# Rotary embedding of the first block's attention: the exchange of halves by a permutation product, or by transfers within SBUF

## The reference, cut to what matters

```python
def apply_rotary(t, cos, sin):
    c = cos[:, :, None, None, :]
    sn = sin[:, :, None, None, :]
    tf = t.astype(jnp.float32)
    t1, t2 = jnp.split(tf, 2, axis=-1)
    return jnp.concatenate([t1 * c - t2 * sn, t2 * c + t1 * sn], axis=-1).astype(t.dtype)

def diff_attention(q, k, v, lam):
    ...
        scores = jnp.einsum('bqhcd,bkhcd->bhcqk', q[:, q_lo:q_hi], k[:, :q_hi],
                            preferred_element_type=jnp.float32) * scale
        ...
        probs = jax.nn.softmax(jnp.where(causal, scores, -jnp.inf), axis=-1)
        weights = probs[:, :, 0] - lam * probs[:, :, 1]
        outs.append(jnp.einsum('bhqk,bkhe->bqhe', weights.astype(v.dtype), v[:, :q_hi]))
```

## Time and profile before

| | |
|---|---|
| median of three executions | 3582.28 us |
| span of the profiled execution | 3593.5 us (the page gives no time around the span) |
| PE busy | 3218.1 us, 90% |
| DVE busy | 1427.9 us, 40% |
| ACT busy | 1130.1 us, 31% |
| attention of the first block | about 30 to 300 us of the span |
| 134 to 212 us, three heads | PE 26.00 of 26.00 us in each, at granted clock 1.00 |

### The profile page before, as it was taken

How to read it: one execution, slowest core, us unless ns; L and a number is a source line. 1 busy time by engine, 2 the same in 40 slices (tenths; PEclk the granted TensorE clock), 3 DMA queues, 4 the chain that set the end, 5 groups by cost and what they waited for, 6 DMA issues and landing times. The chain is left out here.

```text
span 3593.5 us, 42107 instructions
## 1 busy us (share of the span) xinstructions
PE 3218.1 (90%) x16329; PEld 2285.4 (64%) x16329; DVE 1427.9 (40%) x2352; ACT 1130.1 (31%) x1954; POOL 282.2 (8%) x280
## 2 busy tenths in 40 slices
PE   7999999999597877887885989899999998979999
PEld 5777888878333333333334857778887856868887
DVE  6772567743420000000003665443323557353332
ACT  4673676742100000000003243232223334232222
POOL 0000332200000000000000001300000000400000
PEclk9999999999799999999997997999999997989999
DMA  5222222222999999999996200033323300023332
GB/s 119 60 66 77 71 71 71 71 74 97 366 425 428 427 428 427 427 428 427 428 424 181 65 12 4 15 98 94 98 96 92 92 12 4 1 88 94 99 96 93
DMA packets 356679, 606.19 MB, mean 169 GB/s; under 512 B 72416, under 2 KB 306688, under 8 KB 331776
## 3 DMA queue, kind: packets, MB, share of 16 engines
q1 hardware_dynamic: 346544, 592.69, 44.8%
q0 software_dynamic: 9216, 8.42, 0.7%
q10 hardware_dynamic: 720, 2.36, 0.2%
HBM read 605.49 MB, written 23.07 MB: 175 GB/s over the span
## 5 line engine op out<-in xcount | busy, mean ns | idle before, releaser
L1839 PE MATMUL ex_up<-ex_W,ex_XT 128*64 128x512 f32 x1024 | 259.6, 665 | 80.9 <-DMA ex_W<-in_w_expert_up_dram 80.9
L237 ACT ACTIVATE f_hi<-f_raw 128x1024 fp32r<-128x1024 f32 x148 | 157.0, 1061 | 539.9 <-PE ff_bk L297 539.6
L1839 PE MATMUL ex_gp<-ex_W,ex_XT 128*64 128x512 f32 x1024 | 236.7, 616 | 52.1 <-DMA ex_W<-in_w_expert_gate_dram 50.6
L295 PE MATMUL ff_bk<-h_b_hi,f_hi 128*128 128x512 f32 x704 | 276.6, 393 | 2.8 <-DVE h_b_lo L3768 2.8
L296 PE MATMUL ff_bk<-h_b_lo,f_hi 128*128 128x512 f32 x704 | 276.2, 392 | 0.0
L297 PE MATMUL ff_bk<-h_b_hi,f_lo 128*128 128x512 f32 x704 | 275.9, 392 | 0.0
L246 DVE TENSOR_TENSOR f_lo<-f_raw,f_hi 128x1024 fp32r<-128x1024 f32 x148 | 180.8, 1223 | 231.6 <-ACT f_hi L237 231.6
L1868 PE MATMUL ex_yp<-ex_W,ex_hT 128*64 128x512 f32 x1024 | 226.8, 595 | 33.1 <-DMA ex_W<-in_w_expert_down_dram 18.4
L1882 DVE TENSOR_TENSOR ex_hid<-ex_sg,ex_up 128x512 f32<-128x512 f32 x32 | 22.0, 687 | 583.3 <-PE ex_up L1839 583.3
L1839 PEld LDWEIGHTS ex_up<-ex_W,ex_XT 128*64 128x64 f32 x1024 | 92.0, 152 | 247.8 <-issue 247.8
L1839 PEld LDWEIGHTS ex_gp<-ex_W,ex_XT 128*64 128x64 f32 x1024 | 87.5, 141 | 200.0 <-issue 198.2
(11 more groups left out here) (624 smaller groups left out, 6603.9 us busy)
## 6 DMA issues: line engine op xcount, KB each, us to landing
ex_W<-in_w_expert_gate_dram SPq DMA_DIRECT2D x64, 2048.0 KB, 37.8
ex_W<-in_w_expert_up_dram SPq DMA_DIRECT2D x64, 2048.0 KB, 37.6
ex_W<-in_w_expert_down_dram SPq DMA_DIRECT2D x64, 2048.0 KB, 38.7
b_raw<-in_w_in_dram SPq DMA_DIRECT2D x88, 512.0 KB, 3.8
f_raw<-in_w_gate_up_dram SPq DMA_DIRECT2D x88, 512.0 KB, 3.9
f_raw<-in_w_down_dram SPq DMA_DIRECT2D x44, 512.0 KB, 3.6
m_raw<-in_w_in_dram SPq DMA_DIRECT2D x20, 512.0 KB, 4.0
m_early<-in_w_in_dram SPq DMA_DIRECT2D x20, 512.0 KB, 4.0
```

The costliest lines, as they stand in the source:

```text
L237: a.activation(self.hi[n % self.SLOTS][:, at], self.raw[n % self.RAW][:, at], ACT.Copy).then_inc(self.cast, 1)
L295: pe.matmul(out, a[0], b[0], start=first, stop=False)
L1839: ins = pe.matmul(ps[part[e], :], XT[b][:, q, part[e]], row_view(slots[e], KD)[:, q, :], start=(q == 0), stop=(q == KD - 1))
```

## The change

TensorE's permutation products go. Behind each evacuation of Q or K, ACT waits until its own write is done and issues four DMAs within SBUF, each of 32 partitions by 512 float32 (64 KB): partitions 0 to 31 of `turn[j]` are filled from 32 to 63 of `plain[j]` and so on. Each adds 16 to the semaphore `swapped[j]`, and DVE waits for all four before it multiplies `turn[j]`, now in place in SBUF, by the sine. The sign goes into the table: the frequencies of the lower 32 partitions of each 64 are negated (`freq64_signed`, one more constant column), which turns the sine's sign and leaves the cosine. The bank `aux` now serves V alone, so that its waits are simpler.

```diff
--- before.py
+++ after.py
@@ -65,12 +65,13 @@
     parts["ret_state"] = np.stack([np.exp(lg[2 * b + head_of] * 128) for b in range(2)], 1)
     p1 = np.arange(P)
     parts["freq64"] = (1.0 / (f(10000.0) ** ((2 * (p1 % 32)).astype(f) / f(64)))).astype(f)[:, None]
+    parts["freq64_signed"] = np.where(p1[:, None] % 64 < 32, -parts["freq64"], parts["freq64"])
     parts["freq32"] = (1.0 / (f(10000.0) ** ((2 * (p1 % 16)).astype(f) / f(32)))).astype(f)[:, None]
     parts["rank"] = p1[:, None].astype(f)
     parts["iota"] = np.broadcast_to(c, (P, P))
     parts["expert_slot"] = np.broadcast_to(np.arange(64)[None, :] * float(CAP), (P, 64))
     parts["rw_keep"] = np.broadcast_to((np.arange(T) % 64 != 0)[None, :], (P, T))
-    first = ["ident", "turn64", "neg_wide", "upto", "before", "later", "ones", "freq64", "freq32", "rank", "iota", "expert_slot"]
+    first = ["ident", "turn64", "neg_wide", "upto", "before", "later", "ones", "freq64", "freq64_signed", "freq32", "rank", "iota", "expert_slot"]
     at, where = 0, {}
     for k in first + [n for n in parts if n not in first]:
         where[k] = (at, parts[k].shape[1])
@@ -473,7 +474,8 @@
         sem = lambda n: k.sem("at_" + n)
         scan_loaded, small_loaded, dots_ready, lam_exp = sem("scan_loaded"), sem("small_loaded"), sem("dots_ready"), sem("lam_exp")
 
-        evacuated, aux_ready, aux_roped, roped, v_taken = sem("evacuated"), sem("aux_ready"), sem("aux_roped"), sem("roped"), sem("v_taken")
+        evacuated, aux_ready, roped, v_taken = sem("evacuated"), sem("aux_ready"), sem("roped"), sem("v_taken")
+        swapped = [sem("swapped_q"), sem("swapped_k")]
 
         scores_done, masked, bias_ready, exp_done, w_ready, turned, wt_ready, out_done, out_taken = (sem(n) for n in (
             "scores", "masked", "bias", "exp", "w_ready", "turned", "wt_ready", "out_done", "out_taken"))
@@ -554,18 +556,10 @@
                     if q == KD - 1:
                         ins.then_inc(W.used, 1)
 
-                def half_turn(n):
-                    i, j = n // 3, n % 3
-                    pe.wait_ge(evacuated, n + 1)
-                    if j == 0 and i >= 1:
-                        pe.wait_ge(v_taken, i)
-                    elif j == 1:
-                        pe.wait_ge(aux_roped, 2 * i + 1)
-                    pe.matmul(aux[:], k.c("turn64"), plain[j][:], start=True, stop=True).then_inc(aux_ready, 1)
-
                 def turn_v(i):
                     pe.wait_ge(evacuated, 3 * i + 3)
-                    pe.wait_ge(aux_roped, 2 * i + 2)
+                    if i >= 1:
+                        pe.wait_ge(v_taken, i)
                     for t in range(NT):
                         ins = pe.transpose(aux[:, t * P:(t + 1) * P], plain[2][:, t * P:(t + 1) * P], k.c("ident"))
                     ins.then_inc(aux_ready, 1)
@@ -575,8 +569,6 @@
                     if part == 0 and 1 <= i <= HEADS:
                         turn_v(i - 1)
                     if i < HEADS:
-                        if part >= 2:
-                            half_turn(3 * i + part - 2)
                         for m in range(6 * part, 6 * part + 6):
                             if m % KD == 0:
                                 start_tile(3 * i + m // KD)
@@ -611,11 +603,16 @@
                     if i >= 1 and j < 2:
                         a.wait_ge(roped, 2 * i + j - 1)
                     elif i >= 1:
-                        a.wait_ge(aux_ready, 3 * i)
+                        a.wait_ge(aux_ready, i)
                     a.activation(plain[j][:], acc[n % 2][:], ACT.Copy).then_inc(evacuated, 1)
+                    if j < 2:
+                        a.wait_ge(evacuated, n + 1)
+                        for r in range(0, P, 32):
+                            from_r = r ^ 32
+                            a.dma_start(turn[j][r:r + 32, :], plain[j][from_r:from_r + 32, :]).then_inc(swapped[j], 16)
 
                 def take_v(i):
-                    a.wait_ge(aux_ready, 3 * i + 3)
+                    a.wait_ge(aux_ready, i + 1)
                     if i >= 3:
                         a.wait_ge(out_done, 4 * (i - 3) + 4)
                     a.activation(V[i % 3][:], aux[:], ACT.Copy).then_inc(v_taken, 1)
@@ -723,8 +720,8 @@
                     i, j = n // 3, n % 3
                     v.wait_ge(evacuated, n + 1)
                     v.tensor_tensor(straight[j][:], plain[j][:], k.cos[:], ALU.mult)
-                    v.wait_ge(aux_ready, n + 1)
-                    v.tensor_tensor(turn[j][:], aux[:], k.sin[:], ALU.mult).then_inc(aux_roped, 1)
+                    v.wait_ge(swapped[j], 64 * i + 64)
+                    v.tensor_tensor(turn[j][:], turn[j][:], k.sin[:], ALU.mult)
                     if i >= 3:
                         v.wait_ge(scores_done, 4 * (i - 3) + 4)
                     v.drain()
@@ -3853,7 +3850,7 @@
             k.make_room_for_h("x", h_ctx, "right")
             with ExitStack() as att_ctx:
                 k.make_room_for_rope("1", att_ctx)
-                rope = RopeTable(k, att_ctx, "r1", ap["positions"], "freq64", k.cos, k.sin)
+                rope = RopeTable(k, att_ctx, "r1", ap["positions"], "freq64_signed", k.cos, k.sin)
                 stage_start(k, W, ap["x"], ap["norm_mix_w"][0], rope)
                 rope.signals("r1_rest")
                 stage_attention(k, W, rope, [ap[n] for n in ("lambda_q1", "lambda_k1", "lambda_q2", "lambda_k2")], ap["subln_w"][0], k.x, merged, sig, scan_small)
```

## The result

The changed kernel is slower: 3600.18 us, median of 7 executions (3597.08 to 3603.57), against 3583.80 us for the kernel before in the same comparison (7 executions, 3580.96 to 3593.82). The ratio is 1.0036 with an interval of 1.0024 to 1.0048, that is +12.9 us (8.6 to 17.2) at 3583.8. The forecast was 3583.2, with a range up to 3592.

A forecast was written before the change was run, and what follows sets the result against it. TensorE and a ring of DVE and ACT were taken as almost equally long bounds. Terms -4.7 + 7.9 - 2.3 = +0.9 us on 3582.28 gave 3583.2 us, range 3574.5 to 3592 for 8 in 10.

The forecast's parts named there:

- ring: Loop of DVE and ACT in the attention, from one attT_lo to the next: 26.03 us, with 0.38 us of slack.
- stacked issues: Rival that ACT's issues back up behind each other; 29 us or more between attT_lo starts would show it; 10%.
- (1): Heads 0 to 2, before the ring closes: TensorE bounds, so removing the products gains time, -4.7 us.
- (2): Heads 3 to 7: five passes of the ring with a Q evacuation, each 1.58 us longer, +7.9 us.
- (3): The end: 2.37 us of room before the transposes of head 6's third unit takes over -2.3 us of the delay.
- d: ACT's delay per tensor of Q or K, taken as 1.96 us; the sum in general is 5d - 8.9.
- issues cost ACT little: Rival: issues go out beside ACT's work, d = 0.3, total -7.4 us, time 3574.9 us; chance 10%.
- TensorE is all that counts: Rival: TensorE alone sets the attention's pace, so 13.4 us are won, time 3568.9 us; chance 5%.
- The issues back up: Rival: ACT's issues queue behind each other; with d of 4 us, +11.1 us, time 3593.4 us; chance 10%.
- TensorE's clock: Rival: TensorE, waiting 3.2 us a head, falls to half clock, adding 4.4 us, time 3587.6 us; chance 8%.
- The transfers land late: Rival: transfers land after more than 6.5 us; at 8 us, 11.5 us over five heads, time 3594.7; chance 4%.

The follow-up runs named there:

- e1: The changed kernel with all 64 transfers issued by SP between its weight loads instead of by ACT; ratio to the kernel before 0.9992.
- e3: The changed kernel with no exchange at all, neither products nor transfers; DVE multiplies the plain tile by the sine; ratio to the kernel before 0.9991.
- e6: The kernel before, with attT_lo on DVE moved behind the piece of its turn (weight rest and Q's rotary); ratio to the kernel before 0.9998.
- e5: The changed kernel, ACT still issuing, with attT_lo on DVE moved behind the piece of its turn; ratio to the kernel before 1.0003.
- e10: The changed kernel with SP issuing the transfers of heads 0 to 2 and ACT those of heads 3 to 7; ratio to the kernel before 1.0028.
- e9: The changed kernel with two transfers of 64 partitions per tensor instead of four of 32, not the rotary's exchange; ratio to the kernel before 1.0012.
- e7: e1, SP issuing all transfers, with attT_lo on DVE also moved behind the piece of its turn; ratio to the kernel before 0.9959.
- e4: The kernel before with its products kept, plus 64 transfers issued by ACT into tiles that nothing reads; ratio to the kernel before 1.0047.
- e11: The changed kernel with all 64 transfers issued by GpSimd instead of ACT; ratio to the kernel before 0.9980.
- e12: e11, GpSimd issuing all transfers, with attT_lo on DVE also moved behind the piece of its turn; ratio to the kernel before 0.9960.
- e8: The changed kernel with two of each tensor's four transfers issued by ACT and two by SP; ratio to the kernel before 1.0015.

## Why the prediction was wrong

The mechanism was right: ring and TensorE almost equally long, the issues of Q in the ring, those of K beside it, DVE gapless in its half, no wait for a transfer in the ring, some 3 us of waits a head on TensorE. Its own test, 27.6 us expected and 29 for stacked issues, read 28.24. Wrong were three terms of the sum.

| term | predicted | measured | marks |
|---|---|---|---|
| (1) heads 0 to 2 | -4.7 | -1.65 | mask of unit 9: 108.49, 106.84 |
| (2) five passes | +7.9 | +11.66 | to the fifth attT_lo: 217.03, 227.04 |
| (3) the end | -2.3 | -0.84 | to the last product: 335.71, 344.88 |
| sum | +0.9 | +9.17 | |

(2) *"I take 1.96 us per tensor"* failed. d is 2.57, since an issue takes 0.61, not 0.33 to 0.43. The prices had been read from issues to or from DRAM, the only ones in the trace; transfers within SBUF it did not have. The ring is then 25.65 + 2.57 = 28.22, 2.2 over the old one, so 11.0 for five passes; measured are 2.2 in three of the four distances, 2.48 in the second and 2.58 on the way to the first attT_lo. The second distance is 0.3 longer in e1 and e3 as well (26.05), where ACT issues nothing: against e1 the issues add 2.49 to 2.54 in each of the four. In the prediction's own terms d is 2.67 (b_hi formerly started 0.10 before the evacuation's end), and 5 x 2.67 - 8.9 = +4.5, still "no change": this term alone isn't the miss. The Trainium skill (DMA: Bandwidth & Descriptors, section Anatomy of one DMA) puts a sequencer's dispatch on the GpSimd path at about 50 ns, which the prediction set against the whole issue; the issues here hold their queue ten times as long or more, 0.50 us on GpSimd, 0.59 on SP and 0.61 on ACT at the median.

(1) *"Together -4.7"* failed by 3.0 (by 2.9 between e6 and e5, whose clocks rose together: 107.65 to 105.81): ACT's delay was charged to the ring alone, with nothing for heads 0 to 2 because TensorE bounds there. TensorE waits for ACT there too, for V's evacuation in head 0; ACT's issues take 1 to 2 us in these heads (e10). The rest is missing with SP's issues as well: there the gain is 2.8 us (e6 to e10) to 3.8 (before to e1) where 4.7 was worked out. The late landings in head 0, which the sum didn't hold, are the likely place: the mask of unit 9 is earliest, 103.48, in e9, the one kernel with transfers in which DVE waits for none, 4.2 us before that of e6, whose clock rose 0.5 us earlier. No run separates this part from the rest.

(3) *"TensorE takes over -2.3 of the delay"* failed by 1.5. The 2.37 us between w of unit 26 and its transposes was no slack of the chain. From the fifth attT_lo to the sixth it is 31.06 us before, 31.07 after and 31.04 in e1 and e3, although a product less is in it: a delay goes through this stretch undiminished, and so it does from the sixth to the seventh (24.72 and 24.73). (e5 to e7 can't be set beside them here, since the mark itself is moved.) What -0.84 there is arises behind the seventh attT_lo, 62.90 us ahead of the end before and 62.04 after, and is likely no slack either: each kernel has one stretch at half clock near the end, and TensorE is busy for 5.96 us of it in the kernel before and for 4.09 in the kernel after (the row 295.10 to 301.90 below). Half of the difference is 0.9 us, an estimate, and would be all of it.

The rivals: *issues cost ACT little* and *TensorE is all that counts* are refuted by 2.57 and 28.24. *The issues back up* was the nearest in time, 3593.4 (four issues of 1.18 us and the 0.2 us beside them are 4.9 us, not the 4 it took, which gives 3598), but not in mechanism: no issue in the ring of the kernel after takes 1.18 us, the medians on the three engines are 0.50 to 0.61, and at d = 2.57 the attention already ends 9 us late. *TensorE's clock*: half-clock stretches did come, 3.4 us each at 151.7, 179.1 and 237.1. The table by stretches for two of them and for the one at the end:

```profile
179.10:182.50 3.40, 3.40 (x11) 2.77 (x12) 3.17 (x5) 1.68 (x3) 0.00 (x0) 0.51 0.56 154
237.10:240.50 3.40, 3.40 (x10) 2.63 (x9) 3.14 (x6) 0.16 (x1) 0.00 (x0) 0.50 0.48 141
295.10:301.90 6.80, 4.09 (x11) 3.14 (x12) 2.85 (x4) 1.65 (x3) 0.00 (x0) 0.50 0.05 15
```

The two in the ring's distances cost nothing there: 170.56 to 198.80 holds one and is as long as 198.80 to 227.04, which holds none. *The transfers land late*: up to 6.2 us, in head 0, not in the ring. It didn't show in the end: e1, in which DVE waits 4.1 us for landings, ends at 330.0, and e3, which has no transfers, at 330.1.

Open: the timed difference of the kernel after, 12.9 us, is 3.7 more than the attention's end, inside its interval. Over the seven kernels that issue on ACT it is 4.4 more in the mean (-0.1 in e4 to 7.8 in e5), over the six others (e1, e3, e6, e7, e11, e12) 0.2 (-1.6 to 2.8). That looks like a cost beyond the attention, but no later stage shows it in the single profiles, whose remainders scatter by several us either way. It isn't settled.

## What to carry to other kernels

A transfer whose landing is hidden still costs its issue, here 0.5 to 0.6 us of the engine that issues it, with 64 KB as with 128: put it on a queue on which nothing critical stands behind it, and merge pieces. An engine busy 26.00 of 26.00 can have a ring of others right behind it; work taken from it is worth only the difference, here 0.3 us a head instead of 1.6, until the ring is opened too, and moving one waiting instruction behind independent work did that. The room ahead of one instruction is slack only if nothing else on the same way round waits.

## What the runs showed of the hardware

Issuing a transfer of 64 KB within SBUF takes 0.61 us on ACT, 0.59 on SP and 0.50 on GpSimd, 1.5 to 1.9 times the 0.33 us of the four issues from SBUF to DRAM on ACT's queue; with 128 KB it is 0.57 on ACT (medians). Two on ACT's queue take 1.16 us, and 1.43 when SP issues at the same time (e8). They land in 1.8 us at the least and 2.0 to 3.0 at the median, faster than the small loads of the earlier trace rows. In the kernel after TensorE fell to half clock for 3.4 us behind waits of 1.3 to 1.6 us for w (149.77, 178.00, 234.49), but not behind the same wait at 206.24; in the kernel before, once the clock was full at 31.66, it did so in the attention only from about 287.5. In the ring it cost nothing.
